# The last 14 z and gate blocks of the second block: three fp32r products in place of one fp32 product

## The reference, cut to what matters

```python
xn = rmsnorm(h, norm1_g[l])
proj = xn @ w_in[l]
u_s, x_m, z_m, g_s, g_m = jnp.split(proj, splits, axis=-1)   # 512, 1024, 1024, 1024, 1024 columns
y_s = s5_branch(u_s, ...) @ w_ssm_out[l]
y_m = mlstm_branch(x_m, z_m, ...) @ w_ml_out[l]              # four heads; h = sigmoid(z) * h
mixed = jax.nn.sigmoid(g_s) * y_s + jax.nn.sigmoid(g_m) * y_m
```

## Time and profile before

| | us |
|---|---|
| median of 3 runs (1600.25 to 1605.63) | 1601.89 |
| the profiled execution, its own time | 1597.99 |
| span of that execution, first to last instruction | 1596.2 |
| TensorE busy (98% of the span, 11762 matmul records) | 1569.5 |
| VectorE busy (75%) | 1193.2 |
| ScalarE busy (51%) | 817.6 |
| GpSimd busy (27%) | 429.5 |

### The profile page before, as it was taken

One profiled execution on the slowest core, in us unless ns is written; L12 is line 12 of the kernel. 1 busy time (PEld: TensorE's weight loads), 2 busy tenths in 40 slices (PEclk: granted clock), 3 DMA queues, 4 the chain that ended last, 5 costly groups with the idle time before them and its releaser, 6 DMA issues. The chain is left out here.

```text
span 1596.2 us, 33679 instructions
## 1 busy us (share of the span) xinstructions
PE 1569.5 (98%) x11762; PEld 1445.3 (91%) x11762; DVE 1193.2 (75%) x2303; ACT 817.6 (51%) x1350; POOL 429.5 (27%) x252
## 2 busy tenths in 40 slices
PE   9999999999999999999999999999999999999997
PEld 8998988999999877899999999999999888888886
DVE  7895157887886877356899998778775777777776
ACT  6573345655644742344544445555555555555554
POOL 0615510454420013576779960000000000000000
PEclk9999999999999999999999999999999999999998
DMA  8433443566655221355468885555667777777773
GB/s 313 148 109 117 121 172 121 186 185 186 188 178 187 74 70 44 132 195 162 146 208 232 233 230 178 178 172 179 178 178 234 251 242 235 233 241 230 241 234 116
DMA packets 93100, 289.56 MB, mean 181 GB/s; under 512 B 10336, under 2 KB 27104, under 8 KB 92768
## 3 DMA queue, kind: packets, MB, share of 16 engines
q1 hardware_dynamic: 92736, 287.81, 57.8%
q10 hardware_dynamic: 288, 0.71, 0.2%
HBM read 270.65 MB, written 17.83 MB: 181 GB/s over the span
## 5 line engine op out<-in xcount | busy, mean ns | idle before, releaser
L265 PE MATMUL psum<-arena_parts,ring_parts 128*128 128x256 f32 (+1 forms) x1856 | 522.0, 281 | 0.0
L263 PE MATMUL psum<-arena_parts 128*128 128x256 f32 (+1 forms) x1632 | 468.5, 287 | 6.4 <-DVE arena_parts L1640 2.6
L2825 DVE TENSOR_TENSOR ring_parts<-ring,arena_parts 128x512 fp32r<-128x512 f32 x414 | 280.2, 691 | 156.0 <-ACT arena_parts L2624 93.1
L265 PEld LDWEIGHTS psum<-arena_parts,ring_parts 128*128 128x128 f32 x1856 | 352.6, 190 | 0.0
L263 PEld LDWEIGHTS psum<-arena_parts 128*128 128x128 f32 x1632 | 307.9, 189 | 8.4 <-issue 4.5
L264 PE MATMUL psum<-h_parts,arena_parts 128*128 128x256 f32 x1024 | 286.1, 279 | 0.0
L258 POOL TENSOR_TENSOR ring_parts<-ring,arena_parts 128x1024 fp32r<-128x1024 f32 x81 | 214.9, 2679 | 62.0 <-ACT arena_parts L254 46.6
L2592 PE MATMUL psum<-arena_parts,x_parts 128*128 128x512 f32 x512 | 201.3, 393 | 0.3 <-DVE x_parts L2861 0.3
L2593 PE MATMUL psum<-ring_parts,x_parts 128*128 128x512 f32 x512 | 201.5, 394 | 0.0
L2594 PE MATMUL psum<-arena_parts,x_parts 128*128 128x512 f32 x512 | 201.2, 393 | 0.0
L264 PEld LDWEIGHTS psum<-h_parts,arena_parts 128*128 128x128 f32 x1024 | 193.5, 189 | 0.0
(11 more groups left out here) (556 smaller groups left out, 3178.8 us busy)
## 6 DMA issues: line engine op xcount, KB each, us to landing
ring<-stream SPq DMA_DIRECT2D x473, 512.0 KB, 3.7
kept<-arena SPq DMA_DIRECT2D x128, 128.0 KB, 2.2
arena<-kept SPq DMA_DIRECT2D x32, 512.0 KB, 4.7
arena<-first SPq DMA_DIRECT2D x1, 2144.0 KB, 17.0
arena<-second SPq DMA_DIRECT2D x1, 1632.0 KB, 6.9
out<-arena SPq DMA_DIRECT2D x4, 256.0 KB, 2.1
x<-x_t SPq DMA_DIRECT2D x2, 256.0 KB, 4.7
x<-x_t SPq DMA_DIRECT2D x1, 512.0 KB, 6.1
```

The source lines that it names most:

```text
L263: nc.tensor.matmul(dst, stationary[0], moving[0], start=first, stop=False)
L265: return nc.tensor.matmul(dst, stationary[1], moving[0], start=False, stop=last_one)
L2825: v.tensor_tensor(low[:, s, w], ring[:, s, w], expert_high[:, m % 2, w].bitcast(F32), ALU.subtract)\
```

## The change

Blocks 0 to 9 stay as they are. Blocks 10 to 23 are made by `z_parts`: `three` with the weights' high part in `rounded`, the low part in `low`, and the high and low part of the input. What is added to the other engines' lists:

- ScalarE: `z_part_high(g + 3)` right behind the read of block g, 14 times (128 x 1024, waits for the slot's load). In head 0, behind the read of block 8 and the rounding of block 11, two roundings of the input (128 x 1024 each).
- VectorE: `z_part_low(g)`, 14 times: one behind the first scan of each head, one at the end of each head (10 and 11 in head 0 up to 16 and 17 in head 3), 18 ahead of the last `finish_head`, 19 behind it, 20 to 23 behind the last `finish_y`. At the end of head 0 also two operations that make the low part of the input, in place of `h`, behind a wait for block 9.
- TensorE: each of the 14 blocks waits for its low part, block 10 for the input's low part too.

```diff
+        Z_PARTS, Z_BLOCKS = 10, 24
+        def z_part_high(act, g):
+            part_high(act, rounded, g % 4, z_filled[g % 4] + g // 4)
+
+        def z_part_low(dve, g):
+            s = g % 4
+            dve.wait_ge(S("high"), z_high_base + g - Z_PARTS + 1)
+            nc.vector.tensor_tensor(low[:, s, :], ring[:, s, :], rounded[:, s, :].bitcast(F32), ALU.subtract)\
+                .then_inc(S("vector_gate_low"), 1)
+
+        def z_parts(g):
+            def mats(q, w, b, i):
+                s = g % 4
+                nc.tensor.wait_ge(S("vector_gate_low"), z_low_base + g - Z_PARTS + 1)
+                if g == Z_PARTS:
+                    nc.tensor.wait_ge(S("h_parts"), split["h"] + 6)
+                for k in range(KT):
+                    c = slice(k * P, (k + 1) * P)
+                    ins = three(b[:, 0:T], (rounded[:, s, c], low[:, s, c]), (z_h_high[:, k, :], z_h_low[:, k, :]),
+                                k == 0, k == KT - 1)
+                return ins
+            return mats
+
...
-                project(pe, [g % 4], [z_bank(g)], 1, channels(T, M))
+                project(pe, [g % 4], [z_bank(g)], 1, channels(T, M) if g < Z_PARTS else z_parts(g))
...
+                if Z_PARTS <= g + 3 < Z_BLOCKS:
+                    z_part_high(act, g + 3)
...
                     rotate(2 * hh)
                     scan(2 * hh)
+                    z_part_low(dve, 2 * hh + 10)
...
+                    if hh == 0:
+                        dve.wait_ge(used[(Z_PARTS - 1) % 4], z_filled[(Z_PARTS - 1) % 4] + (Z_PARTS - 1) // 4)
+                        for half in range(2):
+                            ks = slice(4 * half, 4 * half + 4)
+                            dve.wait_ge(S("h_rounded"), split["h"] + 4 + half + 1)
+                            v.tensor_tensor(z_h_low[:, ks, :], h[:, ks, M:TT], z_h_high[:, ks, :].bitcast(F32), ALU.subtract)\
+                                .then_inc(S("h_parts"), 1)
+                    z_part_low(dve, 2 * hh + 11)
+                z_part_low(dve, 18)
                 finish_head(3)
+                z_part_low(dve, 19)
                 finish_y(3)
+                for g in range(20, Z_BLOCKS):
+                    z_part_low(dve, g)
...
                     z_reads(act, 1)
+                    if hh == 0:
+                        for half in range(2):
+                            ks = slice(4 * half, 4 * half + 4)
+                            a.activation(z_h_high[:, ks, :], h[:, ks, M:TT], ACT.Copy).then_inc(S("h_rounded"), 1)
```

More of the change, by code:

```diff
@@ L1532, in z_bank @@
             return g % 2 if g < 8 else 0 if g < 16 else g % 2 * 2
+        Z_PARTS, Z_BLOCKS = 10, 24
+        z_high_base = split["blocks"] + 12 + split["apart"]
+        z_low_base = len(VECTOR_LOWS)
+        z_filled = [pe_at.rounds[s] + 4 for s in range(4)]
+        z_h_high, z_h_low = Area(arena_parts[25344], 29440 - 25344).take(KT, T), h_parts[:, :, M:TT]
+        def z_part_high(act, g):
[17 more added lines that the diff above has]
+            return mats
         def z_products(pe, n):
@@ L2154, in build @@
             split["blocks"] += 12
-            split["h"] += 4
+            split["apart"] += Z_BLOCKS - Z_PARTS
+            split["h"] += 6
             normed["squares"] += 2
```

## The result

The changed kernel takes 1606.82 us in the median (1604.68 to 1610.87), the kernel before beside it 1601.13 (1597.12 to 1605.63): a ratio of 1.0044, 95% interval 1.0032 to 1.0057 (ratios here and below are the record's; the quotient of the two medians is 1.0036). It is slower, by 5.7 us; the forecast was 1599.3, with a range of 1596.0 to 1604.5. The profiled execution took 1606.56 us, with a span of 1604.8, 8.6 more than before; the execution profiled before was 3.1 us faster than its median, the one after within 0.3 us of its own.

A forecast was written before the change was run, and what follows sets the result against it. The heads were taken as a loop of TensorE and VectorE, with TensorE alone setting the pace behind them. The terms 3.0 - 1.2 - 5.2 + 0.8 = -2.6 us gave 1601.89 - 2.6 = 1599.3 us, range 1596.0 to 1604.5.

The forecast's parts named there:

- Between the heads: From head 0 to head 1: three VectorE operations of 1024 elements make it late, +3.0 us at L1842; ends +2.1 and +4.2.
- VectorE comes out of the first scan ... and L1807 and L2103 follow: Head 1: TensorE's sums come 2.9 us late, VectorE reaches L1842 at 604.15 instead of 601.13, and later instructions follow.
- the prediction's own signs of being wrong: Wrong if VectorE's waits for scores or sums don't vanish, turns stay at 21.4 us, or ScalarE's roundings wait for loads inside heads.
- The clock as a rival: Head 1: a 2.1 us wait for the weights lowers the clock, sums end up to 1.7 later, 1600.9 us; chance 0.27.
- Heads 2 and 3: Each head's first block is 0.75 us shorter, less 0.1 for GpSimd starting later: -0.6 each, -1.2 us in all.
- Behind the heads: Blocks 16 to 23: 28.92 us becomes 23.72, -5.2 us; block 23 waits +0.8 us behind ScalarE's list.
- GpSimd first: Behind the scans GpSimd goes first, VectorE loses a whole operation (0.73) in heads 1 to 3; 1604.5 us; chance 0.14.
- Behind the stage: Next stage: nothing seen that would swallow 2.6 us; the rival that a wait there takes the gain, 1601.9 us, chance 0.04.

The follow-up runs named there:

- low part 11 later: Changed kernel with low part 11 moved from the end of head 0 to behind the first scan of head 1; 1603.02 us, ratio 1.0020.
- block 10 again: Changed kernel with the first six of eight k-steps (eighths) of block 10 run once for nothing ahead of the whole block; 1598.45 us, ratio 0.9990.
- The run with `finish_y` moved: Kernel split from block 12, with finish_y ahead of the second rotation and Gelu behind the read of block 21; 1597.20 us, ratio 0.9981.
- split from block 12: Changed kernel with blocks 10 and 11 left fp32, the split begun at block 12 and low parts placed anew; 1603.27 us, ratio 1.0020.
- split from block 18: Only blocks 18 to 23, behind the heads, split; the heads' blocks stay fp32, finish_y and Gelu moved; 1595.12 us, ratio 0.9974.
- work in the waits: Kernel split from block 12, finish_y and Gelu moved, with two k-steps (eighths) of blocks 12 and 14 run once for nothing; 1596.14 us, ratio 0.9977.
- all cures: Changed kernel with six k-steps of block 10 and two of 12 and 14 run once for nothing, finish_y and Gelu moved; 1594.60 us, ratio 0.9969.
- the kernel before made late: Kernel before, all blocks fp32, with three idle VectorE subtractions between the reciprocal of head 0 and the scores of head 1; 1606.70 us, ratio 1.0045.

## Why the prediction was wrong, step by step

**Between the heads: +3.0 forecast, +7.8 measured.** The lateness itself was right. VectorE's three operations took 4.73 us by their rows (4.67 forecast), the weights' wait ended at 598.56 (598.8), block 10 started at 593.32 (593.8). What failed is the step "VectorE comes out of the first scan ... and L1807 and L2103 follow": it let the sums of head 1 run at full speed, 2.9 us late and done when VectorE comes to them at 604.15. They ran at the lower clock, VectorE waited for them until 606.25, and the outputs, inputs and block 11 behind them were slow too. A wait of VectorE for sums was one of the prediction's own signs of being wrong. From L2179 to the next head's scores head 1 takes 617.06 - 598.56 = 18.50 us, head 2 637.88 - 624.33 = 13.55, with the same work and its wait of 0.96 in it: 4.95 us, for which the rows show nothing but the clock. 7.78 - 4.95 = 2.83 is left, against 3.0. The experiments bear this out: with the second wait short (low part 11 later) or filled with work (block 10 again) the sums of head 1 run at 1.00, and in the kernel before a wait of 2.77 put there brings the lower clock.

**The clock as a rival** was named with the right place and the right wait (2.1 us; 2.18 came), and was given a chance of 0.27 and 1.6 us. The chance was set between two waits that were followed by a fall (2.33 and 2.60) and one that wasn't (1.75), as if a length of wait decided. The run with `finish_y` moved fell behind 0.57, that from block 12 held behind 2.38, and in the second trace of the kernel before the waits of 2.34 and 2.60 at 123 and 471 us stand as in the first, with no fall behind them. What decides stays open. And the price was taken from those two waits' aftermath, 3.4 us at the lower level. That is what a fall took where split products followed at once, at 471.00 and in the run with block 10 again. In head 1 the sums, outputs and inputs followed, and the clock stayed low until block 11 was nearly through, 13.7 us in all: the fall cost 4.95 us where 1.6 were put. That a block must come first is not shown: in the split from block 12 the clock was back during the scores of head 3, after some 7 us and ahead of any block. The Trainium skill, page "TensorE: Matmul & The Clock Gate", section "What's actually happening", says that the throttled state is the default and activity releases it. The trace agrees with that only in part: TensorE counts as busy for all of 601 to 614, and yet the clock rises only at 614.

**Heads 2 and 3: -0.6 each forecast, -0.60 each measured.** The wait ahead of L2151 grew to 0.96 (1.2 forecast).

**Behind the heads: -5.2 + 0.8 forecast, -4.3 measured.** Block 23 waited 0.61 (0.8); no other block waited. Low part 19 was done with 0.4 us to spare.

With the measured clock term put in, the sum for the stretch is -2.6 + 4.95 = +2.35; +2.33 was measured. So the other terms of the sum were right together. In the second trace of the changed kernel the clock was low for longer, and the stretch is 4.0 us longer than before.

**GpSimd first** is out: behind the first scan VectorE was first by 0.1 us, in heads 1, 2 and 3 alike.

```profile
602.79 1.72 POOL L1617 TENSOR_TENSOR arena<-arena 128x258 f32<-128x258 f32 x1 [9.03 <-issue]
604.59 0.73 POOL L1618 TENSOR_TENSOR arena<-arena 128x258 f32<-128x258 f32 x1
```

Low part 12 started at 602.70 and took its 1.23 us; GpSimd's operation, 0.09 behind it, took 1.72 in place of 0.73. The Trainium skill, page "SBUF — State Buffer", section "Who interferes with whom", says that the order of issue decides which of the two blocks. By it the price falls on whoever is second, and this row agrees. The prediction's reason against this rival, that the low part stands next in VectorE's own list, held.

**Behind the stage** the forecast saw nothing that would swallow the gain. The next stage took 67.3 to 71.2 us in the traces of all these kernels; in the changed kernel what ends late is one VectorE operation:

```profile
735.36 0.39 PE L263 MATMUL psum<-arena_parts 128*128 128x256 f32 x1 [1.89 <-DVE arena_parts L2348]
```
```profile
732.57 2.73 DVE L2348 TENSOR_TENSOR arena_parts<-arena,arena_parts 128x512 fp32r<-128x512 f32 x1
```

In the first trace of the kernel before the same operation took 0.69 us: it began in a gap between two low parts of GpSimd, 0.09 us ahead of the second. In the second trace it took 2.90 us, and TensorE waited 1.26 for it. A rounding of ScalarE that waits for its load came 23.9 us behind block 23 here and 22.55 in the first trace of the kernel before. Kernels with split blocks show the short stage too (67.3 in the split from block 18, 67.4 in that from block 12) and the long one (71.2 with work in the waits); those with fp32 blocks alone lie between 67.3 and 68.9. So executions differ here by themselves, and whether the change makes the late case likelier (69.5 and 69.4 in its two traces) stays open. The long last stage doesn't belong to the change: it took 358.27 us in the kernel before with `finish_y` moved.

From the end of block 23 to the last matmul the four traces of kernels with fp32 blocks alone took 904.7 to 909.6 us, the ten of kernels with split blocks 906.9 to 915.5. Split blocks as such don't seem to cost that: with the part behind the heads alone and with all cures the medians fell by 5.4 and 6.0 us, and the stretches by 5.2 and 5.3. So of the 5.7 us between the medians the stretch explains 2.3 by the first trace and 4.0 by the second, and the cause of the rest stays open.

## What to carry to other kernels

A new wait of TensorE among short products can cost its own length and then the clock: here 2.2 us of wait and 5 us behind it. Don't price a fall of the clock by how long an earlier one lasted elsewhere; it was 3.4 us where split products followed at once and up to 17.0 in a head. Two cures were cheap here: let TensorE repeat part of a block while it would wait, and take the operation that it waits for (`finish_y`) off the end of a long list. With both, and the Gelu moved, the change gives some 0.3%, and so does splitting only the six blocks behind the heads with `finish_y` and Gelu moved (intervals 0.9959 to 0.9980 and 0.9958 to 0.9989). Moving `finish_y` alone gives 0.1% in the kernel before.

## What was not expected of the hardware

- The lower clock lasted 13.7 us in head 1 (17.0 in the second trace, 13.6 in the kernel before made late) with TensorE busy all the time, 3.4 us where split products followed at once, and some 7 us through the scores of head 3 in the split from block 12.
- The same wait of 1.12 us ahead of block 10 was followed by a fall at once in one kernel, by none in another, and in the changed kernel the fall came behind the next wait. A wait of 2.38 us in front of two split blocks was followed by none. In one kernel, by its mean clocks, it fell in some executions only. Those were the slower ones; but with the clock held the times still spread from 1592 to 1602 us.
- The first trace of the kernel before shows falls at 124 and 472 us. The second shows one within 208 to 216 us instead, though the waits at 123 and 471 us stand there too, and reached head 1's scores 1.35 us sooner (586.65 against 588.00).
